# Value and gate panels of the convolution with tokens as the stationary operand, and one transpose of their product

## What is computed

```python
a = rmsnorm(h, g_mix[i])
z = a @ w_in[i]
q, k, v, cv, cg = jnp.split(z, [D_ATTN, 2 * D_ATTN, 3 * D_ATTN, 3 * D_ATTN + D_CONV], axis=-1)
...
u = cv * jax.nn.sigmoid(cg)
u = lax.conv_general_dilated(u, w_dw, window_strides=(1,), padding=[(CONV_WIDTH - 1, 0)],
                             feature_group_count=D_CONV) + b_dw      # 31 taps, one channel at a time
return jax.nn.silu(layernorm(u, g_ln, b_ln))
```

## Time and profile before

| | us |
|---|---|
| median of three runs | 1189.73 (1189.53 to 1189.9) |
| profiled execution | 1189.45 |
| its span in the profile | 1187.6 |
| PE busy | 1176.5 |
| DVE busy | 728.4 |
| ACT busy | 552.0 |
| POOL busy | 110.8 |

### The profile page before, as it was taken

The page is one execution under the profiler, slowest core; times in us unless marked ns, Lnnn a source line. Parts: engine busy times, 40 slices in busy tenths (PEclk is TensorE's granted clock), DMA queues, the critical chain, the costliest instruction groups (busy, mean ns, idle before and its releaser), DMA issues.

```text
span 1187.6 us, 16327 instructions
## 1 busy us (share of the span) xinstructions
PE 1176.5 (99%) x6102; PEld 1010.6 (85%) x6102; DVE 728.4 (61%) x971; ACT 552.0 (46%) x692; POOL 110.8 (9%) x66
## 2 busy tenths in 40 slices
PE   9999999999999999999999999999999999999996
PEld 9999989988888888888888888888888888888886
DVE  6589767767664555464645556464646555567674
ACT  6544465466464444444343434444343433456552
POOL 0222443335000000000000000000000000000111
PEclk9999999999999999999999999999999999999998
DMA  9655555445557556565555565665656555555541
GB/s 343 204 178 177 178 178 179 163 157 163 193 180 265 192 181 197 188 194 195 179 194 192 179 209 177 194 194 178 209 178 191 198 179 191 196 178 177 186 169 71
DMA packets 111705, 223.30 MB, mean 188 GB/s; under 512 B 3785, under 2 KB 5009, under 8 KB 111408
## 3 DMA queue, kind: packets, MB, share of 16 engines
q1 hardware_dynamic: 111200, 222.08, 56.8%
q10 hardware_dynamic: 464, 0.66, 0.2%
HBM read 220.63 MB, written 2.10 MB: 188 GB/s over the span
## 4 chain that ended last, share of the span: by engine, by line
PE 95%; issue 1%; DVE 1%; ACT 1%; POOL 1%; POOLq 0%; DVEq 0%; ACTq 0%
PE ps L1099 25%; PE ps L1097 25%; PE ps L1098 25%; PE ps L1131 5%; PE ps L1130 5%; PE ps L1132 5%; PE ps L1140 1%; PE ps L1106 0%; PE ps L1280 0%; ACT nT_hi L522 0%; ACT w_hi L490 0%; PE ps L1348 0%; PE ps L1350 0%; PE ps L1385 0%; PE ps L1349 0%
## 5 line engine op out<-in xcount | busy, mean ns | idle before, releaser
L735 DVE TENSOR_TENSOR w_lo<-w_raw,w_hi 128x1024 fp32r<-128x1024 f32 x370 | 458.7, 1241 | 431.0 <-ACT w_hi L490 430.4
L490 ACT ACTIVATE w_hi<-w_raw 128x1024 fp32r<-128x1024 f32 x406 | 430.2, 1060 | 590.9 <-PE ps L1099 494.0
L1097 PE MATMUL ps<-w_hi,nT_hi 128*128 128x512 f32 x864 | 339.2, 393 | 0.0
L1099 PE MATMUL ps<-w_hi,nT_lo 128*128 128x512 f32 x864 | 336.6, 390 | 0.0
L1098 PE MATMUL ps<-w_lo,nT_hi 128*128 128x512 f32 x864 | 336.4, 389 | 0.0
L1099 PEld LDWEIGHTS ps<-w_hi,nT_lo 128*128 128x128 f32 x864 | 162.2, 188 | 33.9
L1098 PEld LDWEIGHTS ps<-w_lo,nT_hi 128*128 128x128 f32 x864 | 162.3, 188 | 33.2
L1097 PEld LDWEIGHTS ps<-w_hi,nT_hi 128*128 128x128 f32 x864 | 162.3, 188 | 33.1
L1097 PE MATMUL ps<-w_hi,oT_hi 128*128 128x512 f32 x480 | 188.1, 392 | 0.0
L1099 PE MATMUL ps<-w_hi,oT_lo 128*128 128x512 f32 x480 | 187.0, 390 | 0.0
L1098 PE MATMUL ps<-w_lo,oT_hi 128*128 128x512 f32 x480 | 186.9, 389 | 0.0
(11 more groups left out here) (162 smaller groups left out, 573.8 us busy)
## 6 DMA issues: line engine op xcount, KB each, us to landing
w_raw<-in_w_gate SPq DMA_DIRECT2D x44, 1024.0 KB, 5.2
w_raw<-in_w_up SPq DMA_DIRECT2D x44, 1024.0 KB, 5.1
w_raw<-in_w_down SPq DMA_DIRECT2D x44, 1024.0 KB, 5.0
w_raw<-in_w_in SPq DMA_DIRECT2D x32, 1024.0 KB, 5.1
w_raw<-in_w_out SPq DMA_DIRECT2D x16, 1024.0 KB, 5.1
w_raw<-in_w_pgate SPq DMA_DIRECT2D x16, 1024.0 KB, 5.0
w_raw<-in_w_in SPq DMA_DIRECT2D x14, 512.0 KB, 9.6
w_raw<-in_w_ple SPq DMA_DIRECT2D x2, 1024.0 KB, 5.6
```

Source lines behind the costliest of these rows:

```text
L490: nc.scalar.activation(slot_of(m)[0], w_raw[:, (m // 2) % RAW, rows], ACT.Copy).then_inc(hi_ready, 1)
L735: nc.vector.tensor_tensor(lo, w_raw[:, (m // 2) % RAW, rows], hi.bitcast(F32), ALU.subtract).then_inc(lo_ready, 1)
L1097: nc.tensor.matmul(banks[t][:, :], x_hi[:, k, rows], w_hi[:, s, k], start=start, stop=False)
L1099: ins = nc.tensor.matmul(banks[t][:, :], x_lo[:, k, rows], w_hi[:, s, k], start=False, stop=stop)
```

## The change

The four value and gate panels take the other form of product, with tokens stationary. ACT takes the sigmoid of the gate banks directly, with `rstd` as a scale per partition (a token is a partition now), into `glu`; DVE multiplies the value banks by `rstd` and by that in one instruction per bank. PE transposes the product, at half 18 for the first pair and at half 34 for the second (`GLU_TURN_AT`), and ACT copies the transposed banks into `u`. The first taps start one half later. `rb` is still made, for the key panels.

```diff
@@ -104,9 +104,10 @@
 
 
 
-CONV_STEPS = [(18, 48), (48, 66), (67, 84)]
+GLU_TURN_AT = [18, 34]
+CONV_STEPS = [(19, 48), (48, 66), (67, 84)]
 CONV_CHUNKS = [(0, 1, 2, 3), (4, 5), (6, 7)]
-CONV_TAP0_AT = [18, 48, 66]
+CONV_TAP0_AT = [19, 48, 66]
 CONV_BEFORE = [0, 4 * (TAPS - 1), 6 * (TAPS - 1), 8 * (TAPS - 1)]
 CONV_OPS = 4 * (TAPS - 1)
 MEAN_AT, VAR_AT, SPREAD_AT = 85, 88, 89
@@ -209,7 +210,7 @@
         masked = part(8432, 2, 384)
         prob = part(9200, 2, 384)
         probT = part(9968, 4, 384)
-        gate_c = part(9968, 4, T)
+        glu = part(9968, TT, NP)
         group_sum = sb("group_sum", [P, 2, T])
         dist = part(8432, 384).bitcast(I32)
         dist4 = part(8816, 384).bitcast(I32)
@@ -293,7 +294,7 @@
         hT_done, nT_hi_ready, nT_ready = sem("hT_done"), sem("nT_hi_ready"), sem("nT_ready")
         sq_ready, sum_ready, msq_ready, rstd_ready = sem("sq_ready"), sem("sum_ready"), sem("msq_ready"), sem("rstd_ready")
         rb_spread, rb_ready, q_scale_ready = sem("rb_spread"), sem("rb_ready"), sem("q_scale_ready")
-        gate_c_ready, u_ready = sem("gate_c_ready"), sem("u_ready")
+        gate_c_ready, glu_turned, u_ready = sem("gate_c_ready"), sem("glu_turned"), sem("u_ready")
         conv_step, tap0_ready, conv_added = sem("conv_step"), sem("tap0_ready"), sem("conv_added")
         mean_ready, centered, dev_squared, dev_added, var_ready = sem("mean_ready"), sem("centered"), sem("dev_squared"), sem("dev_added"), sem("var_ready")
         ln_spread, ln_scaled, ln_silu, convT_hi_ready, convT_ready = sem("ln_spread"), sem("ln_scaled"), sem("ln_silu"), sem("convT_hi_ready"), sem("convT_ready")
@@ -584,6 +585,21 @@
                                          ACT.Copy).then_inc(pleT_hi_ready, 1)
                 if 8 < m <= WO_A and m % 8 == 0 and IN_PANELS[m // 8 - 1] in ("q0", "q1", "v1"):
                     take_panel(m // 8 - 1)
+                for g in range(2):
+                    if m == 16 * (g + 1):
+                        sc.wait_ge(half_done, m)
+                        sc.wait_ge(rstd_ready, 1)
+                        if g:
+                            sc.wait_ge(glu_turned, g)
+                        for t in range(TT):
+                            nc.scalar.activation(glu[:, t], LOW[1][t][:, :], ACT.Sigmoid, scale=rstd[:, 0, t:t + 1]).then_inc(gate_c_ready, 1)
+                    if m == GLU_TURN_AT[g]:
+                        sc.wait_ge(glu_turned, g + 1)
+                        sc.wait_ge(pad_ready, 1)
+                        for b in range(2):
+                            ins = nc.scalar.activation(u[:, 4 * g + 2 * b:4 * g + 2 * b + 2, PAD:PAD + T],
+                                                       HIGH[g][b][:, :].rearrange("p (c t) -> p c t", c=2), ACT.Copy)
+                        ins.then_inc(u_ready, 1)
                 for g in range(3):
                     if m == CONV_TAP0_AT[g]:
 
@@ -592,16 +608,10 @@
                         sc.wait_ge(taps_ready, 1)
                         if g:
                             sc.wait_ge(conv_step, CONV_BEFORE[g])
-                        else:
-                            sc.wait_ge(pleT_ready, 1)
                         for c in CONV_CHUNKS[g]:
                             ins = nc.scalar.activation(conv_sum(c), u[:, c, 0:T], ACT.Identity, scale=taps[:, c, 0:1],
                                                        bias=par[:, B_DW + c:B_DW + c + 1])
                         ins.then_inc(tap0_ready, 1)
-                for g in range(2):
-                    if m == 16 * (g + 1):
-                        sc.wait_ge(panel_read, 2 * g + 2)
-                        nc.scalar.activation(gate_c[:, :, :], gate_c[:, :, :], ACT.Sigmoid).then_inc(gate_c_ready, 1)
                 for hd in range(HEADS):
                     if m == SCORES_AT[hd] + 1:
                         exps(hd)
@@ -847,19 +857,12 @@
 
             def take_panel(q):
 
-                name = IN_PANELS[q]
-                kind, g = name[:-1], int(name[-1])
-                ve.wait_ge(half_done, PAIRED - 1 if q == 0 else 8 * (q + 1))
-                if q == 0:
-                    ve.wait_ge(rb_ready, 1)
-                if name == "k1":
+                ve.wait_ge(half_done, 8 * (q + 1))
+                ve.wait_ge(rb_ready, 1)
+                if IN_PANELS[q] == "k1":
                     ve.wait_ge(scores_ready, 4)
-                if name == "cg1":
-                    ve.wait_ge(u_ready, 1)
                 for b in range(2):
-                    dst = {"k": kT[:, 2 * b:2 * b + 2], "cg": gate_c[:, 2 * b:2 * b + 2],
-                           "cv": u[:, 4 * g + 2 * b:4 * g + 2 * b + 2, PAD:PAD + T]}[kind]
-                    ins = nc.vector.tensor_tensor(dst, pair_of(q)[b][:, :].rearrange("p (c t) -> p c t", c=2), along_tokens(2), ALU.mult)
+                    ins = nc.vector.tensor_tensor(kT[:, 2 * b:2 * b + 2], pair_of(q)[b][:, :].rearrange("p (c t) -> p c t", c=2), along_tokens(2), ALU.mult)
                 ins.then_inc(panel_read, 1)
 
 
@@ -895,16 +898,15 @@
                     ve.wait_ge(rb_spread, 1)
                     nc.vector.tensor_scalar(q_scale[:, :], rstd[:, 0], SCALE, None, ALU.mult).then_inc(q_scale_ready, 1)
                     nc.vector.tensor_copy(rb[:, :], ps[6][:, 0:T]).then_inc(rb_ready, 1)
-                if m == PAIRED:
-                    take_panel(0)
-                if 8 < m <= WO_A and m % 8 == 0 and IN_PANELS[m // 8 - 1][0] in "ck":
+                if 8 < m <= WO_A and m % 8 == 0 and IN_PANELS[m // 8 - 1][0] == "k":
                     take_panel(m // 8 - 1)
                 for g in range(2):
                     if m == 16 * (g + 1) + 1:
-                        ve.wait_ge(gate_c_ready, g + 1)
-                        ve.wait_ge(panel_read, 2 * g + 2)
-                        nc.vector.tensor_tensor(u[:, 4 * g:4 * g + 4, PAD:PAD + T], u[:, 4 * g:4 * g + 4, PAD:PAD + T],
-                                                gate_c[:, :, :], ALU.mult).then_inc(u_ready, 1)
+                        ve.wait_ge(half_done, 16 * (g + 1))
+                        for t in range(TT):
+                            ve.wait_ge(gate_c_ready, 2 * g + t + 1)
+                            ins = nc.vector.scalar_tensor_tensor(glu[:, t], pair_of(2 * g)[t][:, :], rstd[:, 0, t:t + 1], glu[:, t], ALU.mult, ALU.mult)
+                        ins.then_inc(panel_read, 2)
                 for hd in range(HEADS):
                     if m == SCORES_AT[hd]:
                         row_max(hd)
@@ -1102,9 +1104,8 @@
             def first_column(m, k):
 
                 def column(w_part, x_part, opens):
-                    for c in range(4):
-                        ins = nc.tensor.matmul(LOW[m][c // 2][:, (c % 2) * T:(c % 2 + 1) * T], w_part[:, m, k, c * P:(c + 1) * P], x_part[:, k],
-                                               start=opens and k == 0 and c % 2 == 0, stop=False, skip_group_check=True)
+                    for t in range(TT):
+                        ins = nc.tensor.matmul(LOW[m][t][:, :], x_part[:, k, t * P:(t + 1) * P], w_part[:, m, k], start=opens and k == 0, stop=False)
                     return ins
 
                 pe.wait_ge(hi_ready if k else hi_first, m + 1)
@@ -1221,6 +1222,13 @@
                     spread(0, ps[6], 0).then_inc(rb_spread, 1)
                 if m == PAIRED:
                     pe.wait_ge(rb_ready, 1)
+                for g in range(2):
+                    if m == GLU_TURN_AT[g]:
+                        pe.wait_ge(panel_read, 2 * g + 2)
+                        if g == 0:
+                            pe.wait_ge(taps_ready, 1)
+                            pe.wait_ge(pleT_ready, 1)
+                        turn(glu, 0, HIGH[g]).then_inc(glu_turned, 1)
                 for hd in range(HEADS):
                     if m == SCORES_AT[hd]:
                         scores(hd)
@@ -1292,8 +1300,8 @@
                     continue
                 q, k = (m // 8, m % 8) if m >= PAIRED else (m % 2, m // 2)
                 if k == 0 and q >= 3:
-                    pe.wait_ge(panel_read, q - 1)
-                product = tokens_by_columns if IN_PANELS[q][0] == "v" else columns_by_tokens
+                    pe.wait_ge(panel_read, 2 if q == 4 else q - 1)
+                product = columns_by_tokens if IN_PANELS[q][0] in "qk" else tokens_by_columns
                 rows = slice(2 * k, 2 * k + 2)
                 product(m, pair_of(q), nT_hi[:, rows], nT_lo[:, rows], k == 0, k == 7)
             for q0, start, halves, k0 in ((Q_WO_A, WO_A, 2, 0), (Q_WO_B, WO_B, 2, 4), (Q_WO_C, WO_C, 4, HEADS)):
```

## The result

| | us |
|---|---|
| before, median of 12 runs | 1189.42 (1188.98 to 1189.9) |
| after, median of 12 runs | 1192.5 (1190.9 to 1193.08) |
| ratio | 1.0024, 95% interval 1.0015 to 1.0033 |
| after, profiled execution and its span | 1192.57, 1190.7 |

The change makes the kernel 3.1 us slower, which is 0.24%. The forecast was 2.1 us, 1191.8 us, inside 0.2%. The runs after lie 2.2 us apart, those before 0.9 us. Each run was recorded with its mean granted clock: the eight runs after from 1192.24 us up have 0.996, the four from 1190.9 to 1191.88 have 0.997.

A forecast was written before the change was run, and what follows sets the result against it. PE, busy 99% of the span, was taken as the bound. -5.1 + 1.8 + 2.8 + 1.0 = +0.5, plus 1.6 for the clock, gave +2.1 on 1189.73: 1191.8 us, own range 1191.0 to 1192.9, overall range 1189.4 to 1193.4.

The forecast's parts named there:

- form of the matmuls: 32 value and gate halves on PE: 12 matmuls of 512 columns for 24 of 256, 0.16 us shorter each, -5.1 us.
- transposes: Eight transposes per panel pair on PE's queue, 0.88 us, twice, hidden by nothing: +1.8 us.
- first stop: PE at half 18 waits for the first product, made in DVE's step 17 behind its split for half 20: 2.8 us.
- second stop: PE at half 34 waits for the second product, in DVE's step 33 behind the split for half 36: 1.0 us.
- the clock: PE's granted clock falls at half 18, more likely than not: +1.6 us, ends 0 and 2.7.
- the pieces of data it waits for are the same: For the first two halves, in `first_column`: PE's data waits are unchanged, so they count in the -5.1 us.
- The forecast's lower end, 2.4 us: Wait at half 18 from below: 2.4 us if DVE's reciprocal and mask stood after the product and ACT were no later.
- DVE and ACT work, and the taps,: Changed DVE and ACT instructions, and conv taps with one half less to run in: costed at nothing.
- the clock holds: Rival, chance 0.30: both waits of PE, at halves 18 and 34, but no fall of the clock; 1190.2 us.
- the waits are small: Rival, chance 0.05: DVE gets to the product in time, leaving -5.1 + 1.8 = -3.3 us; 1186.4 us.
- The wide matmul that saves little: Rival, chance 0.03: on PE the 512-column form is worth nothing, 1195.3 us; by the skill page's gap, 1194.3 us.
- The chance of slower: Chance 0.25 of a time above 1192.1 us; faster 0.03, within 0.2% 0.72.

The follow-up runs named there:

- experiment 2: Changed kernel with DVE's product one step earlier (steps 16 and 32, not 17 and 33), PE's transposes unmoved: 1187.04 us, ratio 0.998.
- experiment 8: Kernel with DVE's product in steps 16 and 32, each of the two groups of eight transposes issued twice: 1188.88 us, ratio 0.9995.
- experiment 3: Changed kernel with ten constant matmuls that PE runs before it waits for the product at half 18: 1191.29 us, ratio 1.0017.
- experiment 7: Changed kernel with the first product in DVE's step 16, the second left in step 33: 1188.3 us, ratio 0.9991.
- experiment 9: Kernel with DVE's product in steps 16 and 32, and the small transposes one half later (SMALL_AT 11, not 10): 1186.47 us, ratio 0.9975.
- experiment 10: Kernel before the change with the small transposes one half later (SMALL_AT 11, not 10): 1189.44 us, ratio 1.0001.
- experiment 1: Changed kernel with both transposes one half later (halves 19 and 35) and the first taps at 20: 1187.45 us, ratio 0.9984.
- experiment 4: Changed kernel with five constant matmuls in PE's wait at half 18: 1191.26 us, ratio 1.0015.
- experiment 5: Kernel before the change with one added wait, PE at half 18 for the old product of the first pair: 1192.03 us, ratio 1.0023.
- experiment 6: Kernel before the change with PE's added wait for the old product at half 18, filled with eight constant matmuls: 1191.76 us, ratio 1.0021.

## Why the prediction was right, and where its sizes were off

The place and the cause of each term were right; of the five sizes one was right, and four were off by 0.2 to 0.9 us.

| term | forecast | measured | from |
|---|---|---|---|
| form of the matmuls | -5.1 | -4.2 | experiment 2 against before (-2.4), less the transposes |
| transposes | +1.8 | +1.8 | experiment 8 against 2 |
| first stop | +2.8 | +3.0 | experiment 3 against 7 |
| second stop | +1.0 | +1.3 | experiment 7 against 2 |
| the clock | +1.6 | +1.2 | after against experiment 3 |
| sum | +2.1 | +3.1 | 1192.5 - 1189.42 |

- **The number.** The change was forecast 1.0 us too small, nearly all of it in the form; the errors of the stops and of the clock nearly cancel. That 1191.8 us came within 0.7 us of 1192.5 is in part luck: it was counted from 1189.73, 0.3 above the median of twelve runs.
- **The matmuls.** The period of 2.72 us came as worked out. The step that was mis-sized is "the pieces of data it waits for are the same": they are the same, but PE gets to them sooner, and one had no slack. PE waited for the DMA of `in_p` at half 10, where it had not before; experiments 2 and 9 put that at 0.6 us, and experiment 10 shows that the kernel before has nothing to gain there. With the wait out of the way the form gives -4.8 us: experiment 9 against 10 is -3.0, less the transposes. That is the forecast's own lower size; the last 0.3 us to -5.1 stays open. The two halves of `first_column` are not where it all went: from their first matmul to the transposes behind them they take 6.04 us for 6.29, where 0.3 less was forecast, and 6.04 to 6.22 in the eight kept executions of the new form for 6.28 to 6.45 in the four of the old. The first matmul starts at 6.77 for 6.58 in these two profiles, but anywhere from 6.33 to 6.80 in the one form and from 6.45 to 6.79 in the other, so that belongs to the execution.
- **The transposes** were exact, and nothing hid them.
- **The first stop.** Forecast 2.8 us, 2.9 in the profile, 3.0 in the time. That the product's place in DVE's queue, and not the sigmoid or DVE's load, makes it late is shown by experiment 2, where DVE does the same work. How much of it is the split, how much the reciprocal and mask, was not tried; by the rows those two take 0.8 of the 3.0 us from 59.5 to 62.48. Nor was the table load, 1.28 us ahead of the sigmoids. The forecast's lower end, 2.4 us, does not follow from its condition: without reciprocal and mask (0.9 us between the split and the product in rows 12) and with ACT no later (0.2) its own sum gives 1.7.
- **The second stop.** Forecast 1.0 us, 1.1 in the profile, 1.3 in the time.
- **The clock.** It fell as taken, at the first stop only, but not in every execution: by the mean clocks in eight of twelve. Those eight have a median of 1192.7 us, the other four 1191.3, as the filled stop has, so a fall costs 1.4 us and the median of all twelve shows 1.2. In the profiled execution it is 1.6 against the same half in experiment 3 (64.69 to 67.52, 2.8 us).
- **DVE and ACT work, and the taps,** were costed at nothing, rightly: PE's lists of waits in experiments 1 and 2 have none for the product, the copies or the taps.
- **The rivals.** That the clock holds is what the filled stop imitates, 1191.3 us, where 1190.2 was forecast: the form's missing 0.9 us is in there too. That the waits are small is experiment 2, forecast at 1186.4 and measured at 1187.04 once the order was mended. The wide matmul that saves little falls with the rows of 2.72 us, and with it the gap of the Trainium skill ("TensorE: Matmul & The Clock Gate", Back-to-back issue gap) as the price of a half in this kernel: it gives 1.0 us for the 32 halves, against 4.2 measured. The page calls it the gap of an isolated matmul. Its warning that idle gaps between bursts bring the clock back to half (same page, Why this matters for your kernels) is borne out by experiments 3 to 6, for stops shorter than the gaps that it warns of.
- **The chance of slower,** 0.25, was too low for the sum as it came out. The forecast lay 0.3 us under its bound of 1192.1, the measured median 0.4 above it, and the range for the form, -4.8 to -5.1, was too narrow for a change that brings PE to every transfer sooner. The forecast's own range should have begun at 1191.2, not 1191.0, by its terms.

## What to carry to other kernels

When the bounding engine is given a new thing to wait for, follow the queue of the engine that makes it, and ask what each instruction ahead of it waits for, back to the bounding engine. Here the product had all its inputs at 59.5, and DVE was idle, but the product was written behind a split that waited for ACT's split, which stood behind ACT's table load and sigmoids, and behind the reciprocal and mask: it began 3.0 us later. A saving on the bounding engine also moves it ahead of its transfers, so the waits that had just enough slack before are the ones to look at.

## What the runs showed of the hardware

A stop in mid-stream can bring PE's granted clock from 1.00 to 0.50 for some 3.4 us (64.8 to 68.2 in the profile after, about 66.5 to 69.9 in experiment 5), and both times the fall came after PE had started again. Idle times of 0.9 us (experiment 7) and 1.6 us (experiment 4) showed no sign of it in eleven runs each; with 2.0 us it fell in four of eleven runs, by the mean clock, and with 2.7 us in eight of twelve. The same stop costs less if PE is given matmuls of a constant in it: 1191.3 us for 1192.5.

Eight transposes of 128 x 128 cost 0.92 us of PE's time (experiment 8), and halving the number of matmuls at the same number of columns saved 0.16 us of every 2.88.
